# A float32 decoder step on one core: the strips of the first projection read their columns from a 64-byte boundary

## The reference, cut to what matters

```
h = rmsnorm(x) ; z = h @ w_in                       # 2048 -> u,c,b,q,k,v,o,gates,g_a,g_b
conv = causal_dwconv(c * u) ; a = b * conv          # 3 taps over the tokens
hb = mlstm(q, k, v, gates, state)                   # 8 heads, DK 128, DV 256
mix = sig(g_a) * a + sig(g_b) * sig(o) * hb
x = x + mix @ w_out
up = causal_dwconv(rmsnorm(x) @ w_up)               # 2048 -> 2 * 5632
x = x + (silu(up[..., 5632:]) * up[..., :5632]) @ w_down
y = rmsnorm(x)                                      # the meta tokens are dropped
```

## Time and profile before

| | |
|---|---|
| median of 3 runs | 1715.03 us |
| lowest and highest run | 1714.33 and 1716.58 us |
| span of the profiled execution, first to last instruction | 1712.8 us |
| TensorE busy | 1701.5 us, 99% of the span |
| VectorE, ScalarE, GpSimd busy | 1201.3, 766.6, 475.5 us |
| mean granted TensorE clock | 0.997 |

### The profile page before, as it was taken

The page is one execution under the profiler, slowest core; times in us unless marked ns, Lnnn a source line. Parts: engine busy times, 40 slices in busy tenths (PEclk is TensorE's granted clock), DMA queues, the critical chain, the costliest instruction groups (busy, mean ns, idle before and its releaser), DMA issues.

```text
span 1712.8 us, 37176 instructions
## 1 busy us (share of the span) xinstructions
PE 1701.5 (99%) x13726; PEld 1694.9 (99%) x13726; DVE 1201.3 (70%) x1902; ACT 766.6 (45%) x914; POOL 475.5 (28%) x501
## 2 busy tenths in 40 slices
PE   9999999999999999999999999999999999999997
PEld 8999999999999999999999999999999999999997
DVE  5775957667595866759688877777555777777554
ACT  6544435353443535444444544544333333333443
POOL 4422414242151424215333222222000222222220
PEclk9999999999999999999999999999999999999998
DMA  8788786868778686877766656666666666666663
GB/s 204 177 232 197 198 210 156 224 164 229 181 198 214 152 227 157 231 187 198 191 176 181 189 173 181 177 180 173 182 181 181 179 176 180 174 182 175 183 176 119
DMA packets 591165, 318.80 MB, mean 186 GB/s; under 512 B 17684, under 2 KB 585988, under 8 KB 588988
## 3 DMA queue, kind: packets, MB, share of 16 engines
q1 hardware_dynamic: 578564, 292.99, 64.1%
q10 hardware_dynamic: 10448, 21.57, 4.8%
q0 software_dynamic: 2064, 2.92, 0.8%
HBM read 305.09 MB, written 12.78 MB: 186 GB/s over the span
## 4 chain that ended last, share of the span: by engine, by line
PE 99%; ACT 0%; DVE 0%; POOL 0%; issue 0%; ACTq 0%; POOLq 0%
PE strip L1494 63%; PE strip L1499 32%; PE aux L1372 1%; PE aux L1380 1%; PE strip L1424 0%; PE aux L1553 0%; PE aux L1444 0%; PE strip L1437 0%; PE aux L1583 0%; PE aux L1582 0%; PE aux L1596 0%; PE strip L1372 0%; PE aux L1588 0%; PE aux L1587 0%; PE aux L1580 0%; PE aux L1579 0%
## 5 line engine op out<-in xcount | busy, mean ns | idle before, releaser
L960 DVE TENSOR_TENSOR w_lo<-w_raw,w_hi 128x1024 fp32r<-128x1024 f32 x556 | 721.1, 1300 | 317.9 <-ACT w_hi L701 317.3
L701 ACT ACTIVATE w_hi<-w_raw 128x1024 fp32r<-128x1024 f32 x557 | 586.5, 1059 | 765.9 <-PE strip L1499 740.6
L1494 PE MATMUL strip<-xh,w_hi 128*128 128x266 f32 (+2 forms) x3424 | 865.5, 286 | 0.0
L1494 PE MATMUL strip<-xl,w_hi 128*128 128x266 f32 (+2 forms) x3424 | 864.6, 286 | 0.0
L1494 PEld LDWEIGHTS strip<-xh,w_hi 128*128 128x128 f32 x3424 | 644.8, 188 | 0.2
L1494 PEld LDWEIGHTS strip<-xl,w_hi 128*128 128x128 f32 x3424 | 644.0, 188 | 0.0
L1499 PE MATMUL strip<-xh,w_lo 128*128 128x266 f32 (+2 forms) x3424 | 494.5, 286 | 0.0
L1499 PEld LDWEIGHTS strip<-xh,w_lo 128*128 128x128 f32 x3424 | 451.4, 188 | 0.4 <-DVE w_lo L960 0.4
L1494 PE MATMUL strip<-hh,w_hi 128*128 128x264 f32 x704 | 176.2, 285 | 0.0
L1494 PE MATMUL strip<-hl,w_hi 128*128 128x264 f32 x704 | 174.8, 283 | 0.0
L672 POOL TENSOR_TENSOR gg<-sg,cz 128x264 f32<-128x264 f32 x44 | 57.4, 1304 | 414.9 <-ACT sg L915 414.9
(11 more groups left out here) (324 smaller groups left out, 1334.9 us busy)
## 6 DMA issues: line engine op xcount, KB each, us to landing
w_raw<-in_w_in SPq DMA_DIRECT2D x256, 512.0 KB, 4.4
w_raw<-in_w_up SPq DMA_DIRECT2D x176, 512.0 KB, 4.1
w_raw<-in_w_down SPq DMA_DIRECT2D x64, 512.0 KB, 4.0
w_raw<-in_w_out SPq DMA_DIRECT2D x32, 512.0 KB, 4.5
w_raw<-in_w_down SPq DMA_DIRECT2D x32, 384.0 KB, 3.4
out<-c_st ACTq DMA_DIRECT2D x8, 1024.0 KB, 7.1
c_st<-in_state_mlstm_C ACTq DMA_DIRECT2D x7, 1024.0 KB, 10.4
rb<-scratch_rows ACTq DMA_DIRECT2D x8, 270.0 KB, 5.0
```

Source lines behind the costliest of these rows:

```text
L701: act.activation(w_hi[:, slot, :], w_raw[:, slot, :], ACT.Copy).then_inc(hi_done, 1)
L960: v.tensor_tensor(w_lo[:, slot, :], w_raw[:, slot, :], w_hi[:, slot, :].bitcast(f32), ALU.subtract).then_inc(lo_done, 1)
L1494: pe.matmul(bank[b][:, 0:c1 - c0], w_hi[:, slot, w], xt[:, k0 + k, c0:c1], start=(first and k == 0 and t == 0), stop=False)
```

## The change

The rows of `xh` and `xl` become XW = 288 columns long (1152 bytes, a multiple of 64), and the data begins at column X0 = 4 of a row in the first phase. Every strip that began at column M0 now begins at C0, so that it reads 268 columns instead of 266, and its first column is column 16 of a row, byte 64. The strips with 268 columns begin there too (before: byte 48 of the row). k and v begin at column 4, byte 16 (before: byte 0). `take` reads the wanted 266 columns from the third column of the bank on. In the up projection the columns still begin at column 0 of a row; only the pitch differs. The rows of `mh` and `ml` become MW = 268 columns long (1072 bytes, a multiple of 16), of which 266 are read. The hand-made layout moves with it: the base of the region, the offsets of four tensors, and `x3`, which now lies over tensors of an earlier phase. No instruction and no wait is added or taken away.

```diff
+    MW = (NM + 3) // 4 * 4
+    X0 = 16 - C0
+    XW = (X0 + NT + 15) // 16 * 16
...
-        xh = sb("xh", [P, KT, NT], f32r)
-        xl = sb("xl", [P, KT, NT], f32r)
+        xh = sb("xh", [P, KT, XW], f32r)
+        xl = sb("xl", [P, KT, XW], f32r)
...
-        base = (nc.sbuf_base + 223) // 512 * 512 + 288
+        base = (nc.sbuf_base + 479) // 512 * 512 + 32
...
-        mh = at("mh", [P, KT, NM], f32r)
-        ml = at("ml", [P, KT, NM], f32r)
+        HEAD = 2 * KT * MW * 4
+        mh = at("mh", [P, KT, MW], f32r)
+        ml = at("ml", [P, KT, MW], f32r)
+        cursor[0] = HEAD
...
-        x3 = at("x3", [P, 2, NF])
...
-        cursor[0] += (448 - cursor[0]) % 512
+        cursor[0] += (64 - cursor[0]) % 128
...
+        x3 = at("x3", [P, 2, NF])
...
-                act.activation(xh[:, k, :], x_bank[k % 6][:, 0:NT], ACT.Copy, scale=vecs[:, k:k + 1])\
+                act.activation(xh[:, k, X0:X0 + NT], x_bank[k % 6][:, 0:NT], ACT.Copy, scale=vecs[:, k:k + 1])\
...
-            def take(u, b, out, c0, width):
+            def take(u, b, out, c0, width, from_c=C0):
...
-                v.tensor_tensor(out, bank[b][:, 0:width], rbc[:, c0:c0 + width], ALU.mult).then_inc(evacuated, 1)
+                v.tensor_tensor(out, bank[b][:, c0 - from_c:c0 - from_c + width], rbc[:, c0:c0 + width], ALU.mult).then_inc(evacuated, 1)
...
-                c0 = M0 if s == 0 else 0
+                c0 = C0 if s == 0 else 0
...
-                strip(n * 16 + s, n * HEAD_U + 2 * s, 2 * s, s % RING, xh, xl, c0, c1, (), between)
+                strip(n * 16 + s, n * HEAD_U + 2 * s, 2 * s, s % RING, xh, xl, X0 + c0, X0 + c1, (), between)
...
-                    mix_strip(n, s, M0 if s == 0 else 0, NT, spread_r if first and s == 2 else None)
+                    mix_strip(n, s, C0 if s == 0 else 0, NT, spread_r if first and s == 2 else None)
...
-                    wide = (s - 4) % 6 < 2
-                    mix_strip(n, s, C0 if wide else M0, NT)
+                    mix_strip(n, s, C0, NT)
```

More of the change, by code:

```diff
@@ L223, in hybrid_decoder_step @@
         rtok = at("rtok", [P, 3])
-        assert cursor[0] <= 2 * KT * NM * 4
-        cursor[0] = 2 * KT * NM * 4
+        assert cursor[0] <= HEAD
+        cursor[0] = HEAD
         tmp_s = at("tmp_s", [P, KT, NS])
@@ L228, in hybrid_decoder_step @@
         gex = at("gex", [GR, NT])
-        assert cursor[0] <= 2 * KT * NM * 4 + 2 * NS * DV * 4
-        cursor[0] = 2 * KT * NM * 4 + 2 * NS * DV * 4 + 22 * 1024 - 32
+        assert cursor[0] <= HEAD + 2 * NS * DV * 4
+        cursor[0] = HEAD + 2 * NS * DV * 4 + 41 * 512 - 32
         sq_junk = at("sq_junk", [P, D])
-        cursor[0] = 2 * KT * NM * 4 + 2 * NS * DV * 4 + 30 * 1024 - 32
+        cursor[0] = HEAD + 2 * NS * DV * 4 + 57 * 512 - 32
         diag = at("diag", [P, 3, P])
@@ L997, in _ @@
                 v.wait_ge(xh_done, k + 1)
-                v.scalar_tensor_tensor(out=xl[:, k, :], in0=x_bank[k % 6][:, 0:NT], scalar=vecs[:, k:k + 1],
-                                       in1=xh[:, k, :].bitcast(f32), op0=ALU.mult, op1=ALU.subtract)\
+                v.scalar_tensor_tensor(out=xl[:, k, X0:X0 + NT], in0=x_bank[k % 6][:, 0:NT], scalar=vecs[:, k:k + 1],
+                                       in1=xh[:, k, X0:X0 + NT].bitcast(f32), op0=ALU.mult, op1=ALU.subtract)\
                                         .then_inc(xl_done, 1)
@@ L1216, in back @@
                             v.wait_ge(mixed, j + 1)
-                            v.tensor_scalar(mh[:, bass.ds(j, 1), :].rearrange("p a t -> p (a t)"), mx[:, :], 1.0, None,
+                            v.tensor_scalar(mh[:, bass.ds(j, 1), 0:NM].rearrange("p a t -> p (a t)"), mx[:, :], 1.0, None,
                                             ALU.mult).then_inc(mix_split, 1)
                             v.wait_ge(mix_split, j * 2 + 1)
-                            v.tensor_tensor(ml[:, bass.ds(j, 1), :].rearrange("p a t -> p (a t)"), mx[:, :],
-                                            mh[:, bass.ds(j, 1), :].rearrange("p a t -> p (a t)").bitcast(f32),
+                            v.tensor_tensor(ml[:, bass.ds(j, 1), 0:NM].rearrange("p a t -> p (a t)"), mx[:, :],
+                                            mh[:, bass.ds(j, 1), 0:NM].rearrange("p a t -> p (a t)").bitcast(f32),
                                             ALU.subtract).then_inc(mix_split, 1)
@@ L1288, in _ @@
                             step(n, 8, u0, 2 * q)
-                            take(n * 8 + (u0 + 2 * q + 1), q, zs[:, z, :], 0, NM)
+                            take(n * 8 + (u0 + 2 * q + 1), q, zs[:, z, :], 0, NM, 0)
                             v.wait_ge(evacuated, out_of(n * 4 + (s0 + q)))
@@ L1423, in first_hi @@
                     for t, xt in enumerate((xh, xl)):
-                        mm = pe.matmul(bank[s][:, 0:NT - c0], w_hi[:, 2 * s + k // KU, w], xt[:, k, c0:NT],
+                        mm = pe.matmul(bank[s][:, 0:NT - c0], w_hi[:, 2 * s + k // KU, w], xt[:, k, X0 + c0:X0 + NT],
                                        start=(k == 0 and t == 0), stop=False)
@@ L1437, in first_lo_part @@
                     mm = pe.matmul(bank[s][:, 0:NT - c0], w_lo[:, 2 * s + h, (k - h * KU) * P:(k - h * KU + 1) * P],
-                                   xh[:, k, c0:NT], start=False, stop=(last and k == KT - 1))
+                                   xh[:, k, X0 + c0:X0 + NT], start=False, stop=(last and k == KT - 1))
                 return mm
@@ L1443, in gates @@
                     for t, xt in enumerate((xh, xl)):
-                        mm = pe.matmul(aux[1][0:GM, 0:NT], gws[:, k, :], xt[:, k, :], start=(k == 0 and t == 0),
+                        mm = pe.matmul(aux[1][0:GM, 0:NT], gws[:, k, :], xt[:, k, X0:X0 + NT], start=(k == 0 and t == 0),
                                        stop=(k == KT - 1 and t == 1))
```

## The result

| | before | after |
|---|---|---|
| median, 21 runs each | 1714.77 us | 1716.82 us |
| lowest to highest | 1713.55 to 1716.58 us | 1716.15 to 1719.29 us |
| span of the profiled execution | 1712.8 us | 1716.6 us |

The ratio is 1.0013, interval 1.0007 to 1.0018: 2.05 us slower, between 1.2 and 3.1. The prediction said 1712.9, within 1708.8 to 1716.5. It had the wrong sign, and the time lies just above its range.

The account below looks back on a forecast made before the run. It took TensorE's pace from one matmul to the next as the bound; -1.8 (first-phase strips) and -0.3 (out projection), the rest 0, summed to -2.1 us, so 1715.0 became 1712.9 us, range 1708.8 to 1716.5.

Parts of the forecast that it names:

- part (4): Up projection, 176 units at the new pitch of 1152: taken as 0, bounds -4.2 and +1.8 us.
- The four stretches: Stretches of the kernel before, read for pace by width and starting byte; claimed to show 16 bytes to matter, not 64.
- The bound against: Up projection: a place as bad as 8 bytes off, +0.010 a unit in 176 units, +1.8 us.
- rival D: Up and k/v strips: the new pitch is worse, +1.8 + 0.5 - 2.1 = +0.2, 1715.2 us; chance 0.07.
- Part (1): First phase's 266-column strips, 144 units, reading 268 from a multiple of 16 at 2.9525 a unit: saves 1.8 us.
- Rival B: Heads' strips: the price belongs to the place in the head, not the address; 1714.9 us, chance 0.13.
- the wide strips: First phase's 268-column u and c strips, 64 units, moved from byte 48 or 16: taken as 0, bound 0.2 us.
- Part (2): Out projection, rows all beginning on 16 bytes, 32 units from 2.964 to 2.954: saves 0.3 us.
- Part (3): k and v strips, 46 units beginning at byte 16 with pitch 1152: taken as 0, bounds +0.5 and -0.6 us.
- Parts (5) and (6): `take` reading two columns further on, and moved tensors: no longer take, no added wait, down strips cost the same.
- Rival A: Up projection and k/v strips: 64-byte alignment counts, between -3.5 and -6.9, about 1709.5 us; chance 0.25.
- Rival C: First phase's strips: two more columns paid in full, alignment gives nothing, +3.3 us, 1718.3; chance 0.10.

Follow-up runs that it names:

- e1: Kernel before with only the xh and xl pitch raised to 1152 bytes, tensors of the region moved as in the changed kernel: ratio 1.0014.
- g2: Changed kernel with the up projection's 266 columns starting at column 14, byte 56: up halves 260.91 and 260.48 us, 2.960 a unit.
- e2: Kernel before, pitch 1120, with the first phase's narrow strips reading 268 columns from byte 48 or 16, region moved: ratio 0.9995.
- i3: Kernel before with ten turns of the first up half written out, each behind a small matmul of 8 to 128 columns: 2.953 or 2.954 a unit.
- j2: Kernel before with a small matmul of 8 to 128 columns, by head, before strip 6: eight units 23.79 to 23.81 us with it.
- g1: Changed kernel with the up projection reading 268 columns instead of 266 from byte 0, pitch 1152: 2.973 us a unit in both halves.
- g3: e2 with the up projection also reading 268 columns from byte 0 or 32, pitch 1120: 2.973 us a unit in both halves.
- h1: Pitch 1152, 268 columns from byte 48, plus small matmuls before strip 6 (8 to 128 columns) and second up half (8): heads 2.947 or 2.980, half 259.39 us.
- i1: Pitch 1152, 268 columns from byte 48, mh and ml as before, 8-column matmul before second up half: 1710.56 us, ratio 0.9976 to kernel before.
- h4: Pitch 1152, 268 columns from byte 48, with only one 128-column matmul added, before the second up half: that half 262.31 us.
- i4: Pitch 1152, 268 columns from byte 48, ten first-up-half turns written out behind small matmuls: 2.947 a unit in eight, 2.980 at 80 and 112 columns.

## Why the prediction was wrong

**The step that failed** is part (4): "The four stretches show 16 bytes to matter and not 64, so I take 0." Those stretches differ in width, in pitch and in what stands ahead of them as well as in the 16 bytes, and none has a pitch of 1152. The up projection's 176 units went from 2.953 to 2.973, +3.5 us, from the pitch (e1). The bound against, +1.8, was half of it; it was taken from 8 bytes off as the worst place, and g2 shows that byte 56 is cheaper at this pitch. The prediction had named this as the way in which it is most easily wrong, with 0.02 us a unit, and gave rival D 0.07. D is what came at the up projection, about twice as large as its price; its other half (k and v dearer) was false: they became 0.06 a head cheaper.

**Part (1)**, 1.8 us with 2.9525 a unit, was the second failure. The strips came to 2.960, 0.09 us a head, 0.7 in all. The pace was read from the later two wide strips and the slower first two were set aside. The alignment wasn't the cause of what was saved: e1 saves it without. Rival B ("the price belongs to the place in the head") was nearer: e2 has 2.940 and 2.974 for one form in one head. That the heads gave 1.8 us in all, the number of the forecast, is luck: the wide strips, taken at 0 with a bound of 0.2 us, gave 0.07 a head, 0.6 in all, and k and v, taken at 0, gave 0.06 a head.

**Part (2)**, -0.3, was +0.27 (2.963 to 2.973 a unit). In e1, with 266 columns a row, the out projection stays at 94.84. Rows that begin on 16 bytes were a loss there. **Part (3)** was forecast 0 and gave 0.5 us (46 units), within its bound. **Parts (5) and (6)**: TensorE waits for no queue and for no `take`, as said. But the moved layout isn't free: the last down half takes 128.95 us in the three kernels with the layout of before (that kernel, i3 and j2) and 129.45 in e1 and e2, whose region is moved, while the first down half stays at 127.98. The units behind the transposes of the output take 3.04 us there, where the layout of before has 2.99, 3.01 and 3.04 in turn. Which of the moved tensors does it wasn't tried, and neither was whether it is the entry again.

**Rival A** (64 bytes count, to the good) is refuted by the up projection. (Its working has a slip: the middle of -3.5 and -6.9 gives 1709.8, not 1709.5.) **Rival C** (columns paid in full) is refuted by g1 and by the heads; at 1120 bytes g3 pays 0.020 a unit, about the 0.023 that C has, so its price appears in one form. The formula that stands beside C is given in the Trainium skill (TensorE: Matmul & The Clock Gate, Back-to-back issue gap) for an isolated matmul, not for a stream of weight loads and matmuls, which the prediction left out; 268 columns took 122.5 to 124.2 ns here (2.940 to 2.980 / 24), above its 114.

The Trainium skill (SBUF — State Buffer, Specifications (TRN2)) has cachelines of 16 bytes and a penalty for each cross to a new line. The prediction had its lines counted as equal, 67 and 67, with part (1) worth nothing by that rule; the strips moved 0.005 us a unit. For the up projection the count of lines is the same before and after, and the trace differs by 0.020: by that rule alone the loss could not be seen.

What is shown: for columns that begin at byte 0 of a row, the new pitch makes the loss in the kernels as they are entered; it is not the distance of xh and xl; one place modulo 64 for all rows is not slow in itself; the form with 268 columns from byte 48 has two paces and the entry picks. What stays open: why one matmul follows another after 123.1 or 123.9 ns (2.953 and 2.973 / 24), and whether the pitch does it by itself or because it puts every row at byte 0: no run has every row there at another pitch, and with this pitch the starts at bytes 56 and 48 gave 2.960, and 2.947 or 2.980. Many of the unit's paces lie on a grid (2.940, 2.947, 2.953, 2.960, 2.973, 2.980, steps of 0.0067 us or two of them), and the 2.963 of the kernel before is units of 2.960 and 2.967 in turn. It looks as if something with a period of its own were locked to the stream; that is an argument and no run names it.

## What to carry to other kernels

Where TensorE is the bound and the matmuls follow each other without a wait, read the pace from the starts of equal blocks in the chain, stretch by stretch, and multiply each stretch's difference by its count: here an edit made for 144 units changed 176 others, and these decided the sign. A pace read at one place is not a property of the form until the stretch has been entered in other ways. A sweep within one kernel (the same body behind eight or ten small matmuls of different width) costs one run and shows whether it is; the spread here, 0.034 us a unit or 1.1%, is larger than what alignment was meant to bring.

## What was unexpected of the hardware

- The same loop body on the same addresses ran at 2.947 or 2.980 us a unit (24 matmuls) over a whole phase, picked by one matmul ahead of it: 8 columns 2.947, 128 columns 2.980 (h1 and i1 against h4). The widths that pick the slow pace differ from place to place: 80, 96 and 128 in the heads (h1), 80 and 112 but not 96 or 128 in the first up half (i4).
- At a pitch of 1152 bytes 268 columns from byte 48, well entered, are faster (2.947) than 266 from byte 0 (2.973). In the up projection two more columns from the same start cost nothing at 1152 bytes (g1) and 0.020 a unit at 1120 (g3).
- A pitch of 1136 bytes, 16 less, made both the heads (76.08 against 75.73) and the up halves (262.65 against 262.13) slower than 1152.
